# A mixer block of one core: weights of the second half split during the first, and the convolution divided among three engines

## The chip, the cores and the metric

The kernel runs on one core of one Trainium2 chip. Its time is the device time of one execution in microseconds. Before the change the runs took 3051.74, 3052.08 and 3052.36 us; their median is 3052.08.

## What is computed

The reference is two residual blocks over 2048 tokens of 1024 features, in float32.

```python
x = x + gate * gla_mixer(rmsnorm(x, g) * (1 + scale) + shift)     # first block, linear attention in chunks of 64
x = rmsnorm(x, final_g)
u = rms_norm(h) * (1 + scale) + shift                             # second block; h is the first one's output
p = u @ w_in                                                      # q, k, v, z of attention, a and g of the convolution, z of the convolution
attn = attend(rope(q), [k_ctx, rope(k)], [v_ctx, v]) * silu(z_a)  # 8 heads of 64, 2304 keys
y = depthwise_conv31(a * sigmoid(g)) + conv_b                     # 512 channels, 31 taps along the tokens
conv = (silu(layer_norm(y)) @ w_pw + b_pw) * silu(z_c)
h = h + gate * (concat(attn, conv) @ w_out)
```

## The kernel before

The program runs six phases one after the other, each with its own tiles and semaphores and a barrier ahead of it: modulation, the linear attention (`gla_block`), context keys, the projections (`projections`), the attention (`attention`) and the output. A matrix product in float32 is made of three products of rounded values: w_hi by a_hi, w_hi by a_lo and w_lo by a_hi, where hi is the rounded value and lo what is left. ScalarE rounds (`w_hi` from `w_raw`), GpSimd subtracts (`w_lo`).

**Turns.** Tokens go in four blocks of 512 (`NB`). In a block, each turn of TensorE multiplies one tile of weights, 1024 x 128, by the block: 24 matmuls of 512 columns into one of two banks. The linear attention has 32 turns a block (0 to 7 for q and k, 8 to 15 for v, 16 to 23 for the gate, 24 to 31 for the output), the projections 22 (0 to 7 for a and g of the convolution in turn, 8 to 13 for q, k and v, 14 to 21 for the two z). ScalarE evicts the bank of turn j, which TensorE needs again in turn j+2 (waits on `proj_out` and on `evac`).

**Weights.** In block 0 of both phases SyncE loads a raw tile, the two parts are formed, and SyncE stores them to scratch (`keep_split`). In later blocks it loads the pair of tile n from scratch into one of three buffers, two turns ahead (`load_pair`, L324 and L1088), once turn n-3 is done. All of SyncE's transfers stand in one queue written out by hand, in order of the turns, with the waits of each between them.

**Convolution.** Four groups of 128 channels. The gate (L1358) writes u into `conv_in`; VectorE then makes 31 taps a group (`tap`, L1330 the first, L1333 the others), each one multiply-add of 128x528 into `conv_acc`. `TAPS_OF_TURN` deals the 124 taps of a block to its turns; 28 are carried into the first four turns of the next block, and in the end behind the last turn. VectorE also forms u of the next block in turns 9 to 19 (L1317, L1319 the rounded part, L1321 the rest), does q's norm and rotation, and gates z. GpSimd adds the squares of h (L1059) and two products of q (L1161, L1167).

**Attention.** 32 steps, one for each head and block of queries, of 18 key tiles each. TensorE makes scores (L1598, L1599), the scores for the maxima of the next step (`piece`, L1558, four banks, 20 pieces in groups of four), and the weighted sum of v (L1573). ScalarE takes the exponentials (L1662). VectorE takes the maxima from PSUM (L1694), writes them to `mz` (L1703), splits q (L1687) and adds the last two of eight pairs to the denominator (L1711) and halves it (L1715). GpSimd adds the first six pairs (L1543, 128x1024). ScalarE's and GpSimd's steps are loops with registers for most steps.

## Time and profile before

| | us |
|---|---|
| median of the three runs | 3052.08 |
| the profiled execution, its own time | 3046.05 |
| its span, first to last instruction | 3044.2 |
| TensorE busy | 2615.0 (86%) |
| VectorE busy | 1814.0 (60%) |
| ScalarE busy | 1092.1 (36%) |
| GpSimd busy | 793.3 (26%) |
| mean granted clock of TensorE | 0.928 of full |

Busy times are unions of the instructions of an engine. Engine names of the rows are PE (TensorE, with PEld for its weight loads), DVE (VectorE), ACT (ScalarE), POOL (GpSimd) and SP (SyncE); SPq is SyncE issuing a transfer. In a row of a timeline x13 are 13 instructions in a row, and the bracket holds the idle time ahead of them and what ended it. A number like L1333 is a line of the kernel before.

### The profile page before, as it was taken

The page shows a single profiled execution, that of the slowest core. Times are in us where ns is not written, and L with a number is a line of the kernel's source. Part 1 is how long each engine was busy: PE and PEld are TensorE (multiplying, and loading weights), DVE is VectorE, ACT ScalarE, POOL GpSimd, SP SyncE. Part 2 cuts the span into 40 slices and gives each one's busy share as a digit, 9 for nine tenths or more (in the row PEclk, how much of TensorE's full clock was granted, in tenths as well). Part 3 has the DMA queues.
Part 4 walks back from the last instruction along what each step waited for, and adds up shares of the span by engine and source line. Part 5 has one row for each costly group of instructions (what it writes and reads, how often), then busy time and mean ns, then how long its engine had stood idle before and what let it go on. Part 6 is the DMA issues. An engine that isn't in the chain of part 4 may idle for free. (4 is left out here: it accounts for less than half of the span.)

```text
span 3044.2 us, 35493 instructions
## 1 busy us (share of the span) xinstructions
PE 2615.0 (86%) x11647; PEld 1777.7 (58%) x11647; DVE 1814.0 (60%) x2830; ACT 1092.1 (36%) x1875; POOL 793.3 (26%) x365
## 2 busy tenths in 40 slices
PE   8599899999999962767989797299999999975998
PEld 1277677777777751645767675144454445433776
DVE  0106423533532524698898888677777777746564
ACT  0234433333332413241414132144454445433332
POOL 0033300000000101532111111166566656642000
PEclk9799999999999985888999999599999999987999
DMA  8275664454355341746555554411111111124334
GB/s 307 94 250 167 225 218 143 155 186 164 134 193 193 101 152 59 258 150 228 188 185 202 183 204 157 99 27 26 33 26 28 27 33 26 28 71 149 117 117 148
DMA packets 230581, 414.82 MB, mean 136 GB/s; under 512 B 19607, under 2 KB 112397, under 8 KB 230204
## 3 DMA queue, kind: packets, MB, share of 16 engines
q1 hardware_dynamic: 230096, 413.13, 40.9%
q8 instruction: 70, 1.15, 0.2%
q14 instruction: 51, 0.42, 0.0%
q10 hardware_dynamic: 364, 0.13, 0.0%
HBM read 306.87 MB, written 97.94 MB: 133 GB/s over the span
## 5 line engine op out<-in xcount | busy, mean ns | idle before, releaser
L1694 DVE TENSOR_REDUCE att_mx<-att_bank_m 128x1 f32<-128x512 f32 (+1 forms) x640 | 365.5, 630 | 111.6 <-PE att_bank_m L1558 107.6
L1662 ACT ACTIVATE att_p_f<-att_bank_s 128x512 f32<-128x512 f32 x576 | 317.7, 598 | 288.0 <-PE att_bank_s L1599 281.0
L412 PE MATMUL gla_bank_g<-gla_a_hi,gla_w_hi 128*128 128x512 f32 x1024 | 416.1, 406 | 4.1 <-POOL gla_w_lo L365 3.1
L412 PE MATMUL gla_bank_g<-gla_a_hi,gla_w_lo 128*128 128x512 f32 x1024 | 403.7, 394 | 0.0
L412 PE MATMUL gla_bank_g<-gla_a_lo,gla_w_hi 128*128 128x512 f32 x1024 | 403.7, 394 | 0.0
L1543 POOL TENSOR_TENSOR att_den<-att_den,att_p_f 128x1024 f32<-128x1024 f32 x160 | 379.4, 2371 | 34.1 <-ACT att_p_f L1662 22.0
L1333 DVE SCALAR_TENSOR_TENSOR proj_conv_acc<-proj_conv_in,proj_conv_w,proj_conv_acc 128x528 f32<-128x528 f32 x508 | 383.2, 825 | 0.3
L1196 PE MATMUL proj_bank_g<-proj_u_hi,proj_w_hi 128*128 128x512 f32 x704 | 302.8, 430 | 74.9 <-DMA proj_w_lo<-scratch_w_lo 37.8
L1196 PE MATMUL proj_bank_g<-proj_u_lo,proj_w_hi 128*128 128x512 f32 x704 | 283.5, 403 | 0.0
L1196 PE MATMUL proj_bank_g<-proj_u_hi,proj_w_lo 128*128 128x512 f32 x704 | 282.6, 401 | 0.0
L1573 PE MATMUL att_bank_o<-att_p_f,att_v 128*64 128x512 f32 x1152 | 268.4, 601 | 0.0
L1598 PE MATMUL att_bank_s<-att_q_a,att_k_a 128*128 128x512 f32 x576 | 258.8, 449 | 1.0 <-ACT att_q_b L1645 1.0
L1599 PE MATMUL att_bank_s<-att_q_b,att_k_b 65*128 65x512 f32 x576 | 230.2, 400 | 0.0
L412 PEld LDWEIGHTS gla_bank_g<-gla_a_hi,gla_w_hi 128*128 128x128 f32 x1024 | 195.3, 191 | 55.6 <-issue 14.2
L412 PEld LDWEIGHTS gla_bank_g<-gla_a_hi,gla_w_lo 128*128 128x128 f32 x1024 | 194.9, 190 | 42.6
L412 PEld LDWEIGHTS gla_bank_g<-gla_a_lo,gla_w_hi 128*128 128x128 f32 x1024 | 195.6, 191 | 38.1 <-issue 0.7
L1196 PEld LDWEIGHTS proj_bank_g<-proj_u_hi,proj_w_hi 128*128 128x128 f32 x704 | 138.6, 197 | 125.2 <-DMA proj_w_lo<-scratch_w_lo 41.0
L1598 PEld LDWEIGHTS att_bank_s<-att_q_a,att_k_a 128*128 128x128 f32 x576 | 109.7, 190 | 136.9 <-issue 105.4
L372 POOL TENSOR_TENSOR gla_ke<-gla_qk,gla_tmp 128x512 f32<-128x512 f32 x16 | 20.8, 1297 | 631.8 <-ACT gla_tmp L610 631.8
L778 DVE COPY gla_v_tok<-gla_bank_t 128x512 f32<-128x512 f32 x32 | 22.1, 691 | 266.6 <-PE gla_bank_t L519 266.6
L1558 PE MATMUL att_bank_m<-att_k_a,att_q_c 64*128 64x512 f32 (+1 forms) x640 | 121.9, 433 | 60.7 <-ACT att_k_a L1634 57.7
L1196 PEld LDWEIGHTS proj_bank_g<-proj_u_lo,proj_w_hi 128*128 128x128 f32 x704 | 138.9, 197 | 35.8 <-issue 8.2
(322 smaller groups left out, 4195.4 us busy)
## 6 DMA issues: line engine op xcount, KB each, us to landing
gla_w_hi<-scratch_w_hi SPq DMA_DIRECT2D x96, 512.0 KB, 3.7
gla_w_lo<-scratch_w_lo SPq DMA_DIRECT2D x96, 512.0 KB, 4.7
proj_w_hi<-scratch_w_hi SPq DMA_DIRECT2D x66, 512.0 KB, 3.9
proj_w_lo<-scratch_w_lo SPq DMA_DIRECT2D x66, 512.0 KB, 5.3
scratch_w_hi<-gla_w_hi SPq DMA_DIRECT2D x32, 512.0 KB, 3.2
scratch_w_lo<-gla_w_lo SPq DMA_DIRECT2D x32, 512.0 KB, 4.2
mod_wslab<-in_ada_w SPq DMA_DIRECT2D x6, 2048.0 KB, 11.2
mod_wslab<-in_w_mod SPq DMA_DIRECT2D x6, 2048.0 KB, 8.1
```

Source lines behind the costliest of these rows:

```text
L372: pool.tensor_tensor(ke[:], qk[:, 1, :, tok(t)], tmp[:, 1, :].rearrange("p (h i) -> p h i", h=4), ALU.mult).then_inc(qs_pool, 1)
L412: last = pe.matmul(banks[s % 2][:], w[:, k, :], a[:, k, :], start=(k == 0 and n == 0), stop=(k == KT - 1 and n == 2))
L778: dve.tensor_copy(v_tok[:, :, tok(j)], T[j % 2][:].rearrange("p (t i) -> p t i", t=NT)).then_inc(v_copied, 1)
L1196: last = pe.matmul(G[j % 2][:], w[:, k, :], a[half][:, k, :], start=(k == 0 and n == 0), stop=(k == KT - 1 and n == 2))
L1333: dve.scalar_tensor_tensor(conv_acc[:, c, :], src, conv_w[:, c, k:k + 1], conv_acc[:, c, :], ALU.mult, ALU.add).then_inc(taps, 1)
L1543: pool.tensor_tensor(den[s][:], pair(0) if j == 1 else den[s][:], pair(j), ALU.add).then_inc(den_pool, 1)
L1558: pe.matmul(M[p % MBANKS][:, 0:width], q_c[s][rows, P * qt:P * (qt + 1)], k_a[g][rows, TB * n:TB * n + width], start=True, stop=True).then ...
L1573: last = pe.matmul(O[HD * half:HD * (half + 1), :], v[g][:, 2 * j + half, :], p_f[:, 2 * j + half, :], start=(j == 0), stop=(j == NPR - 1))
L1598: pe.matmul(S[kt % SBANKS][:], k_a[g][:, keys], q_a[s][:], start=True, stop=False)
L1599: pe.matmul(S[kt % SBANKS][:], k_b[g][:, keys], q_b[s][:], start=False, stop=True).then_inc(s_done, 1)
L1662: act.activation(p_f[:, kt, :], S[kt % SBANKS][:], ACT.Exp, scale=float(HD) ** -0.5).then_inc(p_done, 1)
L1694: dve.reduce_max(mx[:, qt, n:n + 1], M[p % MBANKS][:, 0:min(TB, KEYS - TB * n)], AX_X).then_inc(mx_read, 1)
```

## The change

Four things change. (1) The 22 tiles of the second block's input weights are rounded, their remainders formed and both stored to scratch during blocks 1 to 3 of the linear attention, one tile in every second turn from 0 to 14 (8, 8 and 6 tiles), through one buffer each (`w2_hi`, `w2_lo`). The projections load all their weights from scratch, into four buffers, on ScalarE's queue. (2) Of the four channel groups VectorE keeps two, 62 taps a block, of 512 columns and 528 in the last block. GpSimd takes group 0 in the projections, a multiplication and an addition for each tap. Group 3 is gated into `vraw` and stored as `conv_u`; in the attention ScalarE multiplies it by a tap's weight, four 512-wide parts a step, and GpSimd adds 128x2048. (3) ScalarE writes u_hi. (4) Block 3 no longer forms u for a block that follows. The steps of ScalarE and GpSimd in the attention are written out.

```diff
 gla_block
+    LATER_EVERY, LATER_PER = 2, 8
+    def later_tile(b, j):
+        n = LATER_PER * (b - 1) + j // LATER_EVERY
+        return n if b and j >= 0 and j % LATER_EVERY == 0 and j < LATER_EVERY * LATER_PER and n < len(IN2_COLS) else None
...
+        w2_hi, w2_lo = sb("w2_hi", [P, KT, P], F32R), sb("w2_lo", [P, KT, P], F32R)
...
+                def load_later(m):
+                    if m >= 2:
+                        sp.wait_ge(w2_rest, UP + m - 1)
+                    else:
+                        sp.wait_ge(w_rest, UP + NW - 1 + m)
+                    sp.dma_start(w_raw[m % 2][:], w_in2[:, :, IN2_COLS[m]:IN2_COLS[m] + P]).then_inc(w_landed[m % 2], 16)
+                def keep_later(m):
+                    sp.wait_ge(w2_rest, UP + m + 1)
+                    for part, tile in (("w2_hi", w2_hi), ("w2_lo", w2_lo)):
+                        sp.dma_start(d[part][m], tile[:].rearrange("p k n -> p (k n)").bitcast(F32)).then_inc(w2_kept, 16)
...
                         load(b * NW + j + 2)
+                        m = later_tile(b, j)
+                        if m is not None:
+                            load_later(m)
+                        m = later_tile(b, j - 3)
+                        if m is not None:
+                            keep_later(m)
...
+                def later_rest(b, j):
+                    m = later_tile(b, j)
+                    if m is not None:
+                        pool.wait_ge(w2_rounded, UP + m + 1)
+                        pool.tensor_tensor(w2_lo[:], w_raw[m % 2][:], w2_hi[:].bitcast(F32), ALU.subtract).then_inc(w2_rest, 1)
...
+                    m = later_tile((n - 1) // NW, (n - 1) % NW)
+                    if m is not None:
+                        act.wait_ge(w_landed[m % 2], UP + 16 * (NW // 2) + 16 * (m // 2) + 16)
+                        act.wait_ge(w2_kept, UP + 32 * m)
+                        act.activation(w2_hi[:], w_raw[m % 2][:], ACT.Copy).then_inc(w2_rounded, 1)
...
 projections
-    NTAP = 4 * TAPS
-    TAPS_OF_TURN = [10, 10, 8] + [0] * 2 + [8] * 5 + [2] * 6 + [8] * 4 + [6] * 2
-    CARRIED = sum(TAPS_OF_TURN[:4])
+    RING = 4
+    NTAP = 2 * TAPS
+    POOL_C, DVE_C, LATE_C = 0, 1, 3
+    TAPS_OF_TURN = [6, 5] + [0] * 4 + [7] * 3 + [5] * 2 + [0] * 5 + [2, 3, 3, 4, 5, 3]
+    CARRIED = sum(TAPS_OF_TURN[:6])
+    POOL_TAPS_OF_TURN = [0] * 2 + [2] * 2 + [1] * 4 + [3, 2, 3, 2, 3] + [1] * 6 + [2] * 2
...
+        def window(b):
+            return CW if b == NB - 1 else TB
...
-                        if b == 0:
-                            keep_split(j)
-                        load(b * NW + j + 2)
...
+                            for k in range(done, done + POOL_TAPS_OF_TURN[j]):
...
+                                    pool.tensor_scalar(prod[:, 0:window(b)], conv_src(b, POOL_C, k), conv_w[:, POOL_C, k:k + 1], None,
+                                                       ALU.mult).then_inc(pool_prod, 1)
+                                    pool.wait_ge(pool_prod, UP + b * (TAPS - 1) + k)
+                                    pool.tensor_tensor(acc, acc, prod[:, 0:window(b)], ALU.add).then_inc(pool_taps, 1)
...
+                def load_pair(n):
+                    j = n % NW
+                    for part, tile in (("w2_hi", w_hi[n % RING]), ("w2_lo", w_lo[n % RING])):
+                        act.dma_start(tile[:].rearrange("p k n -> p (k n)").bitcast(F32), d[part][j]).then_inc(pair_landed[n % RING], 16)
+                for n in range(RING):
+                    load_pair(n)
...
+                def round_u(b, k):
+                    act.wait_ge(hm, UP + b * 8 + k + 1)
+                    act.activation(u_hi[b % 2][:, k, :], hbuf[:, k, :], ACT.Identity, bias=modv[:, 1, k:k + 1]).then_inc(u_done_hi, 1)
...
                         act.wait_ge(proj, UP + b * NW + j + 1)
+                        if b * NW + j + RING < NB * NW:
+                            load_pair(b * NW + j + RING)
...
 attention
+    MUL_AT = (4, 6, 8, 13)
...
+                def tap(k):
+                    pool.wait_ge(conv_mul, UP + NB * (k + 1))
...
+                        pool.tensor_tensor(conv_acc[:].rearrange("p (a b) -> p a b", a=NB), former, conv_prod[:, k % 2, :, :], ALU.add).then_inc(conv_taps, 1)
...
                         pool.tensor_tensor(den[s][:], pair(0) if j == 1 else den[s][:], pair(j), ALU.add).then_inc(den_pool, 1)
-                steps(pool, body)
+                    if i < TAPS:
+                        tap(i)
...
+                    act.activation(conv_prod[:, k % 2, part, :], conv_in[:, k + TB * part:k + TB * (part + 1)], ACT.Copy,
+                                   scale=conv_w[:, k:k + 1]).then_inc(conv_mul, 1)
...
+                        if kt in MUL_AT and i < TAPS:
+                            multiply(i, MUL_AT.index(kt))
```

## Rows read from the trace of the kernel before

**Rows 1.** Stretches, us: PE, PEld, DVE, ACT, POOL busy; PEclk, DMA share, GB/s

```profile
103.00:1127.00 1024.00, 941.98 (x4562) 738.20 (x4561) 397.86 (x762) 370.50 (x697) 128.94 (x66) 0.96 0.51 171
...
1209.00:1433.50 224.50, 155.60 (x578) 114.93 (x578) 184.10 (x209) 66.03 (x88) 84.95 (x37) 0.83 0.60 200
1433.50:1586.00 152.50, 138.41 (x554) 107.54 (x554) 135.06 (x187) 46.80 (x68) 27.33 (x17) 0.95 0.57 191
...
1744.50:1896.00 151.50, 134.24 (x530) 103.90 (x530) 135.11 (x188) 45.99 (x67) 25.30 (x17) 0.93 0.51 177
1896.00:1941.00 45.00, 0.00 (x0) 0.00 (x0) 33.23 (x49) 0.69 (x2) 0.31 (x1) 0.55 0.27 100
1941.00:2720.00 779.00, 750.91 (x3456) 376.54 (x3456) 577.75 (x927) 377.69 (x676) 465.34 (x194) 0.97 0.13 32
```

**Rows 2.** Costliest groups: busy us, mean ns | idle before, releaser

```profile
L1333 DVE SCALAR_TENSOR_TENSOR proj_conv_acc<-proj_conv_in,proj_conv_w,proj_conv_acc 128x528 f32<-128x528 f32 x508 | 383.2, 825 | 0.3
```

**Rows 3.** Waits of TensorE, 1209 to 1433.5: us, times, longest

```profile
PE proj_bank_g L1196 <- POOL proj_w_lo L1146: 23.9, 5, 11.3
```

**Rows 4.** Timelines of the projections, VectorE then GpSimd: start, us, instructions

```profile
1247.44 8.91 DVE L1333 SCALAR_TENSOR_TENSOR proj_conv_acc<-proj_conv_in,proj_conv_w,proj_conv_acc 128x528 f32<-128x528 f32 x13
...
1382.74 9.85 DVE L1333 SCALAR_TENSOR_TENSOR proj_conv_acc<-proj_conv_in,proj_conv_w,proj_conv_acc 128x528 f32<-128x528 f32 x5
...
1174.83 7.08 POOL L1141 MEMSET proj_conv_in<- 128x8380 f32 x1 [134.86 <-POOLq L1061]
...
1250.56 10.91 POOL L1146 TENSOR_TENSOR proj_w_lo<-proj_w_raw,proj_w_hi 128x1024 fp32r<-128x1024 f32 x2 [4.97 <-ACT proj_w_hi L1227]
...
1385.72 1.75 POOL L1161 TENSOR_TENSOR proj_qraw<-proj_qraw,proj_qsin 128x512 f32<-128x512 f32 x1
1387.43 1.77 POOL L1167 TENSOR_TENSOR proj_qraw<-proj_qraw,proj_cos 128x512 f32<-128x512 f32 x1
...
1461.49 1.28 POOL L1059 TENSOR_TENSOR proj_hrs<-proj_hrs,proj_ht 128x512 f32<-128x512 f32 x1 [0.85 <-ACT proj_ht L1232]
```

**Rows 5.** Linear attention: timeline; group of roundings; DMA issues with median landing

```profile
415.34 0.60 ACT L629 ACTIVATE gla_qk<-gla_bank_g 128x512 f32<-128x512 f32 x1 [5.74 <-PE gla_bank_g L412]
...
420.78 0.32 SPq L324 DMA_DIRECT2D gla_w_hi<-scratch_w_hi  x1
421.14 0.43 SPq L324 DMA_DIRECT2D gla_w_lo<-scratch_w_lo  x1
...
L573 ACT ACTIVATE gla_w_hi<-gla_w_raw 128x1024 fp32r<-128x1024 f32 x31 | 32.8, 1057 | 30.3 <-DMA gla_w_raw<-in_gla_w_out 28.5 <-DMA gla_w_raw<-in_gla_w_in 1.7
...
gla_w_lo<-scratch_w_lo SPq DMA_DIRECT2D x96, 512.0 KB, 4.7
scratch_w_lo<-gla_w_lo SPq DMA_DIRECT2D x32, 512.0 KB, 4.2
```

**Rows 6.** Timeline of TensorE: first and last of a turn's 24 matmuls

```profile
1600.68 0.80 PE L1196 MATMUL proj_bank_g<-proj_u_hi,proj_w_hi 128*128 128x512 f32 x1 [3.89 <-DMA proj_w_lo<-scratch_w_lo]
...
1607.38 0.39 PE L1196 MATMUL proj_bank_g<-proj_u_hi,proj_w_lo 128*128 128x512 f32 x1
```

**Rows 7.** Timelines of one attention step: GpSimd, VectorE, TensorE

```profile
2265.63 4.82 POOL L1543 TENSOR_TENSOR att_den<-att_den,att_p_f 128x1024 f32<-128x1024 f32 x2 [0.76 <-ACT att_p_f L1662]
2278.52 2.37 POOL L1543 TENSOR_TENSOR att_den<-att_p_f 128x1024 f32<-128x1024 f32 x1 [8.07 <-ACT att_p_f L1662]
...
2269.18 1.30 DVE L1703 TENSOR_SCALAR att_mz<-att_m 128x4 f32<-128x4 f32 x1
2270.98 1.23 DVE L1711 TENSOR_TENSOR att_den<-att_den,att_p_f 128x1024 f32<-128x1024 f32 x1 [0.50 <-ACT att_p_f L1662]
2272.24 0.69 DVE L1687 TENSOR_TENSOR att_q_a<-att_q_raw,att_q_c 64x512 fp32r<-64x512 f32 x1
...
2274.83 2.48 DVE L1694 TENSOR_REDUCE att_mx<-att_bank_m 128x1 f32<-128x512 f32 x4
...
2278.22 0.73 PE L1558 MATMUL att_bank_m<-att_k_a,att_q_c 64*128 64x256 f32 x4
```

More of the change, by code:

```diff
@@ L28 @@
 GLA_COLS = 3088
+COL_Q, COL_K, COL_V, COL_ZA, COL_A, COL_G, COL_ZC = 0, 512, 640, 768, 1280, 1792, 2304
+IN2_COLS = ([c for i in range(4) for c in (COL_A + P * i, COL_G + P * i)] + [COL_Q + P * i for i in range(4)] + [COL_K, COL_V]
+            + [COL_ZA + P * i for i in range(4)] + [COL_ZC + P * i for i in range(4)])
 VROWS = {}
@@ L1212, in turn @@
                             last.then_inc(vt, 1)
-                        if j == 8:
+                        if j == 8 and b + 1 < NB:
                             sum_h(b + 1)
@@ L1534, in _ @@
                     pool.tensor_tensor(k_b[g][0:HD, :], k_raw[g][0:HD, :], k_a[g][0:HD, :].bitcast(F32), ALU.subtract).then_inc(k_lo_done, 1)
-                def body(i, s, g, before, after):
+                pool.memset(conv_in[:, 0:PAD], 0.0).then_inc(conv_cleared, 1)
+                pool.memset(conv_in[:, PAD + SEQ:], 0.0).then_inc(conv_cleared, 1)
+                def tap(k):
+                    pool.wait_ge(conv_mul, UP + NB * (k + 1))
+                    if k:
+                        pool.wait_ge(conv_taps, UP + k)
+                    former = conv_prod[:, 0, :, :] if k == 1 else conv_acc[:].rearrange("p (a b) -> p a b", a=NB)
+                    if k == 0:
+                        pool.sem_inc(conv_taps, 1)
+                    else:
+                        pool.tensor_tensor(conv_acc[:].rearrange("p (a b) -> p a b", a=NB), former, conv_prod[:, k % 2, :, :], ALU.add).then_inc(conv_taps, 1)
+                for i in range(STEPS):
+                    s = i % 2
                     need(pool, den_sum, i - 1)
@@ L1664, in body @@
                             finish(i - 1, 1 - s)
-                        if kt == 11 and not (isinstance(i, int) and i + 2 >= STEPS):
+                        if kt == 11 and i + 2 < STEPS:
                             round_q(i + 2, s)
```

252 lines of the change are left out of this document (129 added, 123 removed).

## The prediction

> **What bounds the kernel now.** I read the busy times by stage first. In [rows 1] the stretches are, in order: the linear attention (103 to 1127 us), three of the four blocks of the projections (0 from 1209, 1 from 1433.5, 3 from 1744.5 to 1896; block 2 fills the 158.5 us between), what follows their last matmul (to 1941), and the attention (1941 to 2720). The reader is to see three different limits. In the linear attention TensorE is busy 942 of 1024 us. In the attention it is busy 751 of 779. In the projections it is not the limit: a block asks 134 to 138 us of it, but blocks 1 to 3 take 152 to 158 us and VectorE is busy 135 of 152.5 in those shown; block 0 takes 224.5 us, with VectorE busy 184 and TensorE 156. In the 45 us after the last matmul VectorE is busy for 33, with convolution taps. The list of groups says what VectorE does: 508 taps of 128x528, 383 us [rows 2]. The waits of block 0 begin with the remainders of the weights, 23.9 us [rows 3].
>
> Then the timeline of GpSimd and of VectorE, since the change gives GpSimd work in two stages. VectorE alone runs 13 taps in 8.91 us, one each 0.68 us. Beside GpSimd's instructions five take 9.85 us, and GpSimd's 512-wide additions take 1.75 and 1.77 instead of the 1.28 that one takes alone; they start 1.71 apart [rows 4]. So the two take turns: a VectorE instruction that reads two SBUF tensors waits until GpSimd's has ended. One 512-wide GpSimd addition costs a busy VectorE 1.72 - 0.68 = 1.04 us. The same rows show the other outcome: two GpSimd subtractions that met the chain of 13 taps took 10.91 us together and VectorE lost nothing.
>
> **The change, part by part.**
>
> **1. Weights prepared ahead.** Block 0 loses its roundings, remainders, stores and raw loads; its weights come from scratch as in blocks 1 to 3, four tiles ahead, on ScalarE's queue. Its turn then costs what a turn of the other blocks costs.
>
> **2. What this costs in the linear attention.** 22 tiles are treated in turns 0, 2, ... 14 of blocks 1 to 3. By themselves they are a rounding on ScalarE (1.06 us, as in [rows 5]), a subtraction on GpSimd (busy 129 us of the 1024 [rows 1]) and 1.5 MB of transfers, and all could lie beside matmuls. A turn lasts 5.44 us: from the eviction at 415.34, which one turn's end releases, to the pair issue at 420.78, which the next releases [rows 5]. The wait is what costs. w2_hi is one buffer. In turn j ScalarE must see the former tile stored before it rounds, and this stands ahead of its eviction of turn j. SyncE issues that store in its iteration j+1, and ahead of it there stands the wait of the pair load for turn j to be done. So after the end t of turn j come: the pair's two issues and landing, t + 0.36 + 4.7 = t+5.1 [rows 5]; the store's megabyte behind it. Its bounds: it lands 4.2 us after its own issue [rows 5], t+5.5, if it shares nothing, or behind the pair, at the 335 GB/s that 171 GB/s at a share of 0.51 make [rows 1], 3.1 us later, t+8.2. I take the second, since both go through SyncE's queue and the same engines. Then rounding 1.06 and eviction 0.6: t+9.9. TensorE ends turn j+1 at t+5.44 and needs that eviction for turn j+2: it stands 4.5 us. A gap of 3.9 us was followed by a turn of 7.1 us instead of 5.44, its first matmuls at the granted clock's half level of 1.2 GHz [rows 6]; I add 1.5. There are 7, 7 and 5 such waits (the first tile of a block finds its buffer free). Nine in the q and k turns cost 6.0 each; eight in the v turns, which last 0.5 longer, 5.5; the two in turn 14 stand ahead of the decays too (five activations of about 0.6 and a table load, some 4 us of ScalarE), 9.5. Sum 54 + 44 + 19 = **+117**; by the lower bound without a fall of the clock 19 x 1.8 + 8 = +42.
>
> **3. The convolution in the projections.** VectorE keeps two of four channel groups, 62 taps a block for 124: 62 x 0.68 = -42 us; 512 columns for 528 give 1 us more, u_hi on ScalarE 4. What it is busy with falls from 135 to 140 us (the 1.04 for each of 17 GpSimd additions is in that) to about 92. GpSimd gets 31 multiplications and 30 additions a block. The additions take 30 x 1.04 = 31 from VectorE. A multiplication by a scalar is not in this trace. Lower bound: the memset of 8380 columns, 7.08 us [rows 4], 0.84 ns a column, makes 0.43 for 512 and some 0.2 of start, of which VectorE would feel 0.2; upper bound: an addition, 1.04. I take 0.6, between, because it reads one tensor and writes one: 31 x 0.6 = 19. VectorE is back at 92 + 50 = 142. It has next to nothing in turns 2 to 5 (22 us that are TensorE's), and some 130 of the 142 fall into turns 6 to 20, where TensorE asks 6 us a turn and VectorE now 8.7; with the other seven turns at 5.5 that is 168, less the two turns, 11 us, by which TensorE may lead: 157. The Trainium skill, GPSIMD Engine Reference, section 3.1, has a GpSimd loop of at most two operations limited by its ports at 1.03 cycles an element of 1.2 GHz, an estimate of 0.44 us for 512; no row here shows one, and by it the sum would be about 50 us less. So blocks 1 and 2 stay (157 for 152.5 and 158.5). Block 0 becomes one of them: 224.5 - 157 = 67. Block 3 forms no u for a block that isn't there, 24 instructions of 0.5 to 0.75 and the additions and root ahead of them: 20. The carried taps after the last matmul are 11 for 28: 12; the last store is half as long, 2; VectorE, less late there, 4. Sum **-105**. Bounds: TensorE's 134 us in every block, -180; every new GpSimd instruction at 1.04, -50. ScalarE's added pair issues, 0.36 + 0.43 a turn [rows 5], and its rounding of u, a 512-wide operation like the eviction's 0.6, fit beside 5.44 us; if they did not, its evictions would come late (rival d).
>
> **4. The fourth channel group in the attention.** ScalarE multiplies, four times 0.6 us a step, beside matmuls. GpSimd adds 128x2048: 2.41 for 1024 columns (4.82 for two, [rows 7]) make 4.5. It starts when the sixth addition ends, at 2270.5 in the step shown, and fits into GpSimd's 8.07 us of idle. But VectorE has placed its own two-input work in that gap: an addition at 2270.98 (1.23 us), the split of q at 2272.24 (0.69), another addition like the first and a halving of 0.69, then at 2274.83 four maxima in 2.48 us [rows 7]. That GpSimd shuts VectorE out here too is seen at 2269.18: 128x4 elements take 1.30 us, until 2270.48, when GpSimd's pair has just ended. With the tap first, the addition starts at 2275.0, 4.0 us late, the maxima at 2278.8, two of them are read at 2280.1 and four at 2281.3. TensorE's next four score products come at 2278.22 and reuse those banks: 1.9 us, then 0.7, and 0.2 behind: 2.8 us a step. VectorE is busy 578 of 779 us [rows 1], so its later gaps absorb its own lateness before the next tap. 30 taps: 84; the 1 MB store at the end 3: **+87**. Bounds: +3 if VectorE's chain comes first, and +130 if the clock falls each time by 1.5. The longest is half of that in [rows 6], so I add none. The unrolled loops of GpSimd and ScalarE I cost at nothing: ScalarE is busy 378 of 779 us, GpSimd 465 [rows 1], and if instruction fetch stalled one of them it would have to be for microseconds a step.
>
> Sum: 117 - 105 + 87 = **+99**. The profiled execution takes 3046.05 us for a span of 3044.2, so 3145; it is 6 below the median of the runs, 3052.08, which gives **3151 us**.
>
> **The rivals.** (a) Faster: VectorE keeps the port. If a GpSimd instruction is held until VectorE's chain breaks, as the 10.91 us of [rows 4], and the one-input multiplication does not shut VectorE out, the attention loses 3 only and the projections fall to TensorE's 134: 117 - 180 + 3 = -60, **2992 us**. It decides once the projections' gain less the attention's loss passes 120 us. For it: that row; the gap of 8.07. Against: the alternation at 1385 to 1389, and that the tap starts 0.45 us before VectorE's addition. Chance 0.27. (b) The stores land early: item 2 is 42, **3076**. For it: 4.2 us median; against: these had less beside them. 0.12. (c) The clock falls in the attention's waits: +45, **3196**; 0.10. (d) The change does not shorten block 0, because ScalarE, now also issuing, comes late there: +67, **3218**; against it, ScalarE is busy 66 of 224 us there [rows 1]; 0.05. My forecast has the remaining 0.46, with a range of its own of 3095 to 3215.
>
> **The numbers.** What a measurement of this kernel can tell from no change is about 0.2%, 6 us. (a) gives faster 0.27; where (b) meets a projections' gain above mine the two signs cancel, same 0.03; all else is slower, 0.70. The range goes from just under (a) to just over (d), since the bounds of items 3 and 4 reach into both: 2975 to 3225.
>
> **What would show it.** In the linear attention after: a span some 115 longer, TensorE's idle before turns 2, 4, ... by a wait on ScalarE's eviction, and that one on the landing of scratch_w_hi/lo. In the projections: block 0 near 155, VectorE's taps with a mean above 1 us, TensorE's mean granted clock no higher. In the attention: steps 2.8 longer, VectorE's additions of att_den at about 5 us for 1.23 in one of two. The forecast is wrong if the linear attention keeps its 1024 us, if a block falls under 140, or if the attention keeps 779.

## The result, and the profile after

The changed kernel takes 3278.52 us (median of 4 runs, 3275.56 to 3283.29) against 3051.91 us (4 runs, 3049.19 to 3052.36): a ratio of 1.0746, 95% interval 1.0727 to 1.0765. It is slower by 227 us; the forecast was 99 us, with a range for the time of 2975 to 3225 us, and the result lies outside it. The profiled executions are 3283.29 us (span 3281.5) and 3046.05 us (span 3044.2), 237 us apart, and the stages below belong to them.

| from, to | before | after | difference | forecast |
|---|---|---|---|---|
| linear attention, first to last product | 965.1 | 1091.9 | +127 | +117 |
| projections, first product to last tap | 724.4 | 622.2 | -102 | -105 |
| attention, first exponential to the output stage | 756.6 | 975.3 | +219 | +87 |

The rest of the span is 6 us shorter. Two of the three terms come out within 10 us of their forecast; the attention costs 2.5 times its own. The stretches of the kernel after, in the columns of [rows 1] and with its stages (linear attention; projection blocks 0 to 3; what follows their last product; attention):

```profile
101.00:1252.00 1151.00, 981.72 (x4576) 763.10 (x4576) 402.08 (x762) 388.00 (x719) 182.27 (x88) 0.93 0.55 182
1332.40:1487.50 155.10, 138.15 (x554) 105.99 (x555) 116.53 (x116) 55.18 (x80) 126.77 (x78) 0.95 0.54 184
1487.50:1647.50 160.00, 138.57 (x556) 106.93 (x555) 122.78 (x124) 52.05 (x76) 127.58 (x78) 0.95 0.55 191
1647.50:1801.50 154.00, 134.66 (x555) 104.72 (x554) 126.02 (x128) 52.38 (x76) 127.75 (x78) 0.97 0.56 195
1801.50:1943.20 141.70, 132.07 (x553) 103.28 (x551) 101.68 (x107) 38.83 (x56) 114.55 (x71) 0.99 0.53 181
1943.20:1960.00 16.80, 0.03 (x1) 0.00 (x0) 10.64 (x16) 1.08 (x2) 0.00 (x0) 0.58 0.13 48
1960.00:2963.00 1003.00, 897.26 (x3456) 457.85 (x3456) 688.08 (x928) 449.11 (x800) 602.15 (x227) 0.82 0.11 27
```

TensorE is still busy in 897 of the attention's 1003 us, for the same 3456 matmuls that took 751 before. That is the row that says where the time went: only 78 us of the growth are idle time. The granted clock is 0.82 instead of 0.97, and in the linear attention 0.93 instead of 0.96.

**One stall of the linear attention**, timelines of SyncE's queue, ScalarE, GpSimd and TensorE in block 1:

```profile
423.31 0.32 SPq L335 DMA_DIRECT2D gla_w_hi<-scratch_w_hi  x1
423.67 0.43 SPq L335 DMA_DIRECT2D gla_w_lo<-scratch_w_lo  x1
424.15 0.43 SPq L350 DMA_DIRECT2D scratch_w_hi<-gla_w_hi  x1
424.62 0.43 SPq L350 DMA_DIRECT2D scratch_w_lo<-gla_w_lo  x1
...
432.12 1.06 ACT L618 ACTIVATE gla_w_hi<-gla_w_raw 128x1024 fp32r<-128x1024 f32 x1 [9.76 <-DMA scratch_w_lo<-gla_w_lo]
433.08 1.07 ACT L674 ACTIVATE gla_qk<-gla_bank_g 128x512 f32<-128x512 f32 x2
...
433.25 2.37 POOL L398 TENSOR_TENSOR gla_w_lo<-gla_w_raw,gla_w_hi 128x1024 fp32r<-128x1024 f32 x1 [23.15 <-ACT gla_w_hi L618]
...
428.10 0.39 PE L452 MATMUL gla_bank_g<-gla_a_lo,gla_w_hi 128*128 128x512 f32 x1
428.33 0.39 PE L452 MATMUL gla_bank_g<-gla_a_hi,gla_w_lo 128*128 128x512 f32 x1
433.71 0.66 PE L452 MATMUL gla_bank_g<-gla_a_hi,gla_w_hi 128*128 128x512 f32 x1 [5.00 <-ACT gla_qk L674]
...
436.73 0.63 PE L452 MATMUL gla_bank_g<-gla_a_lo,gla_w_hi 128*128 128x512 f32 x1
437.16 0.47 PE L452 MATMUL gla_bank_g<-gla_a_hi,gla_w_lo 128*128 128x512 f32 x1
```

The turn before ends at t = 423.31, where the next pair load goes out. The stores follow at 424.15 and 424.62. ScalarE has been idle for 9.76 us when the second has landed, 8.8 us after t (forecast 8.2), rounds, and only then evicts; TensorE stands 5.0 us (forecast 4.5). Then its matmuls start 0.43 us apart (436.73 to 437.16) and not 0.23 as before the stall (428.10 to 428.33): the granted clock is at its half level for 3.4 us. [rows 5] has the same places without the stall.

**One step of the attention**, timelines of GpSimd, VectorE and TensorE, the places of [rows 7]:

```profile
2307.99 4.91 POOL L1612 TENSOR_TENSOR att_den<-att_den,att_p_f 128x1024 f32<-128x1024 f32 x2 [5.15 <-ACT att_p_f L1753]
2312.84 4.60 POOL L1603 TENSOR_TENSOR att_conv_acc<-att_conv_acc,att_conv_prod 128x2048 f32<-128x2048 f32 x1
...
2311.62 1.31 DVE L1786 TENSOR_SCALAR att_mz<-att_m 128x4 f32<-128x4 f32 x1
2313.42 5.11 DVE L1794 TENSOR_TENSOR att_den<-att_den,att_p_f 128x1024 f32<-128x1024 f32 x1 [0.49 <-ACT att_p_f L1753]
2318.56 0.69 DVE L1770 TENSOR_TENSOR att_q_a<-att_q_raw,att_q_c 64x512 fp32r<-64x512 f32 x1
2319.28 1.23 DVE L1794 TENSOR_TENSOR att_den<-att_den,att_p_f 128x1024 f32<-128x1024 f32 x1
2320.54 0.69 DVE L1798 TENSOR_TENSOR att_den<-att_den 128x512 f32<-128x512 f32 x1
2321.15 2.47 DVE L1777 TENSOR_REDUCE att_mx<-att_bank_m 128x1 f32<-128x512 f32 x4
...
2322.49 0.50 PE L1628 MATMUL att_bank_m<-att_k_a,att_q_c 64*128 64x256 f32 x2 [1.76 <-DVE att_mx L1777]
2323.68 0.50 PE L1628 MATMUL att_bank_m<-att_k_a,att_q_c 64*128 64x512 f32 x2 [0.69 <-DVE att_mx L1777]
```

GpSimd's 128x2048 addition starts 0.58 us ahead of VectorE's, which takes 5.11 us where [rows 7] has 1.23; the next three follow 3.9 us late, then the maxima, and TensorE waits for them twice, 1.76 and 0.69 us. All of this is near the forecast. What was not is in the windows behind it (columns as above):

```profile
2313.00:2324.00 11.00, 8.55 (x38) 4.17 (x38) 10.48 (x9) 5.86 (x11) 6.84 (x2) 1.00 0.18 48
2324.00:2332.00 8.00, 8.00 (x30) 5.77 (x30) 3.77 (x8) 3.98 (x7) 5.10 (x3) 0.57 0.07 16
2332.00:2350.00 18.00, 17.76 (x78) 7.72 (x74) 14.77 (x18) 8.64 (x16) 11.26 (x4) 1.00 0.06 15
2350.00:2366.00 16.00, 13.61 (x40) 7.81 (x42) 8.64 (x16) 5.20 (x10) 9.46 (x4) 0.57 0.09 25
```

After the waits the granted clock is at its lower level of 1.2 GHz for most of 8 us, and it comes back before the next step's waits put it there again. From step 2 to step 31, in the same columns, before and after:

```profile
2016.20:2692.80 676.60, 670.25 (x3132) 335.70 (x3132) 524.68 (x840) 334.08 (x608) 412.67 (x174) 1.00 0.11 28
```

```profile
2037.80:2928.20 890.40, 813.60 (x3134) 416.64 (x3132) 631.25 (x842) 400.88 (x726) 544.39 (x204) 0.83 0.09 21
```

To three digits the second is 0.833: on average 10.2 of the 30.7 us of a step are at the half level, which costs 5.1 us. The waits of TensorE are 2.65 us a step for 0.22. The step before, the added waits and the clock make 23.3 + 2.4 + 5.1 = 30.8, and the step is 30.7. The loss differs from step to step although the waits do not: all 29 steps have two waits of 1.7 to 1.8 and 0.4 to 0.7 us, and they last 29.2 to 32.1 us, with 6.8 to 13.7 us at the half level.

### The profile page after: what moved, and what is told of

Its sections match the earlier page's. It is cut to its first block and busy times, and to the rows that moved or that the text cites. A ratio compares the mean times of both kernels' runs of the same rounds, so it can differ in the third digit from the quotient of the medians.

```text
span 3281.5 us, 34614 instructions
## 1 busy us (share of the span) xinstructions
PE 2776.8 (85%) x11645; PEld 1870.5 (57%) x11645; DVE 1775.2 (54%) x2494; ACT 1173.8 (36%) x2019; POOL 1302.8 (40%) x634
## 5 line engine op out<-in xcount | busy, mean ns | idle before, releaser
L452 PE MATMUL gla_bank_g<-gla_a_hi,gla_w_hi 128*128 128x512 f32 x1024 | 429.4, 419 | 37.6 <-ACT gla_qk L674 33.5
L1233 PE MATMUL proj_bank_g<-proj_u_hi,proj_w_hi 128*128 128x512 f32 x704 | 293.5, 417 | 11.9 <-DVE proj_u_lo L1365 8.4
L1643 PE MATMUL att_bank_o<-att_p_f,att_v 128*64 128x512 f32 x1152 | 303.3, 667 | 0.0
L1668 PE MATMUL att_bank_s<-att_q_a,att_k_a 128*128 128x512 f32 x576 | 293.3, 509 | 1.0 <-ACT att_q_b L1715 1.0
L1669 PE MATMUL att_bank_s<-att_q_b,att_k_b 65*128 65x512 f32 x576 | 260.7, 453 | 0.0
L398 POOL TENSOR_TENSOR gla_w_lo<-gla_w_raw,gla_w_hi 128x1024 fp32r<-128x1024 f32 x22 | 52.1, 2366 | 518.5 <-ACT gla_w_hi L618 518.5
L1376 DVE SCALAR_TENSOR_TENSOR proj_conv_acc<-proj_conv_in,proj_conv_w,proj_conv_acc 128x512 f32<-128x512 f32 (+1 forms) x240 | 246.9, 1093 | 0.0
L1628 PE MATMUL att_bank_m<-att_k_a,att_q_c 64*128 64x512 f32 (+1 forms) x640 | 147.4, 498 | 102.6 <-DVE att_mx L1777 73.3
L1204 POOL TENSOR_SCALAR proj_prod<-proj_conv_in,proj_conv_w 128x512 f32<-128x512 f32 (+1 forms) x120 | 229.1, 1909 | 8.2
L1794 DVE TENSOR_TENSOR att_den<-att_den,att_p_f 128x1024 f32<-128x1024 f32 x64 | 194.1, 3033 | 28.0 <-ACT att_p_f L1753 16.3
L1668 PEld LDWEIGHTS att_bank_s<-att_q_a,att_k_a 128*128 128x128 f32 x576 | 127.6, 222 | 140.0 <-issue 109.9
```

The costliest lines, as they stand in the source:

```text
L452: last = pe.matmul(banks[s % 2][:], w[:, k, :], a[:, k, :], start=(k == 0 and n == 0), stop=(k == KT - 1 and n == 2))
L1204: pool.tensor_scalar(prod[:, 0:window(b)], conv_src(b, POOL_C, k), conv_w[:, POOL_C, k:k + 1], None, ALU.mult).then_inc(pool_prod, 1)
L1233: last = pe.matmul(G[j % 2][:], w[:, k, :], a[half][:, k, :], start=(k == 0 and n == 0), stop=(k == KT - 1 and n == 2))
L1376: dve.scalar_tensor_tensor(acc, conv_src(b, c, k), conv_w[:, c, k:k + 1], acc, ALU.mult, ALU.add).then_inc(taps, 1)
L1643: last = pe.matmul(O[HD * half:HD * (half + 1), :], v[g][:, 2 * j + half, :], p_f[:, 2 * j + half, :], start=(j == 0), stop=(j == NPR - 1))
L1668: pe.matmul(S[kt % SBANKS][:], k_a[g][:, keys], q_a[s][:], start=True, stop=False)
```

## The experiments

Each run is named by its label. Where several attention runs are compared, the figures are a mean over the 29 steps from the start of step 2 to that of step 31, and the waits are TensorE's whole idle time in them. Those timed in rounds have an interval; the others are one execution each, beside the kernel before on the same chip.

### The two costs, each taken away

**e1_no_conv_in_attention**: in the attention neither ScalarE's multiplies nor GpSimd's additions.

> Leaves out channel group 3's whole convolution (the 31x4 multiplies on ScalarE and the 30 additions on POOL in the attention); what is stored for that group is its input. All else is the changed kernel, with the attention's programs of POOL and ScalarE still written out step by step instead of in a loop. Theory P (the addition on POOL keeps VectorE off SBUF, PE waits, and its clock falls to half in each step): the attention's step goes from 30.3 us back to 23.4 us, the attention from 975 to about 760 us, and the kernel from 3278 to about 3062 us. Rival A (the multiplies on ScalarE) expects the same here. Rival L (the cost lies in the programs without a loop, or in the two loads at the attention's start) expects that under half of the 219 us goes: 3170 us or more. My forecast's own size of this part, 87 us, would give 3191 us.

Measured 3070.30 us (ratio 1.0064, 1.0048 to 1.0081); step 23.3 us, clock 1.00, attention 761.7 us. This is theory P's number within 8 us. L is out: the programs without a loop cost nothing a step, and the attention is only 5 us longer than in the kernel before. Half of that is the end, with the 1 MB store (36.2 us from the last step's start, for 33.6 in the kernel before and in e9, which has no such store). The other half is the first step, 25.7 for 22.9 us, and it is not the added loads: e9, which has none of them, takes 25.8 us there. Both have 16 us at the half level in it, where the kernel before has 10.

**e2_addition_after_fold**: the same work, with GpSimd's addition later by one place.

```diff
+                    if i:
+                        pool.wait_ge(den_dve, UP + i * DVE_ADDS)
+                        tap(i - 1)
                     need(pool, den_sum, i - 1)
...
-                    if i < TAPS:
-                        tap(i)
```

> The same 30 additions of 128x2048 on POOL and the same multiplies, but POOL makes the addition of step i at the start of step i+1, once VectorE has folded the denominators, instead of between its own last denominator addition and VectorE's first. VectorE then has nothing but sources in PSUM until the next step's end. Theory P: VectorE's 5.1 us addition is back at about 1.23 us, the step is 23.4 to 24.5 us, the clock in the attention 1.00, the attention 760 to 795 us, the kernel 3060 to 3100 us. Rival Q (POOL has simply too much to do in a step, 18.8 of 23.4 us) and rival A (ScalarE's multiplies) expect the step to stay over 27 us and the kernel over 3180 us.

Measured 3091.34 us (ratio 1.0131, 1.0114 to 1.0148); step 24.0, clock 1.00. 30 additions of 4.56 us are there, nothing is done less, and 187 us are gone: GpSimd's load and ScalarE's multiplies (rivals Q and A) are not the cause, the place of the addition is. Timelines of GpSimd, VectorE and TensorE in one step:

```profile
2210.74 4.56 POOL L1603 TENSOR_TENSOR att_conv_acc<-att_conv_acc,att_conv_prod 128x2048 f32<-128x2048 f32 x1 [4.54 <-DVE att_den L1798]
...
2217.78 12.44 POOL L1615 TENSOR_TENSOR att_den<-att_den,att_p_f 128x1024 f32<-128x1024 f32 x5
...
2210.58 2.48 DVE L1777 TENSOR_REDUCE att_mx<-att_bank_m 128x1 f32<-128x512 f32 x4
...
2228.32 1.93 DVE L1786 TENSOR_SCALAR att_mz<-att_m 128x4 f32<-128x4 f32 x1
2230.34 1.23 DVE L1794 TENSOR_TENSOR att_den<-att_den,att_p_f 128x1024 f32<-128x1024 f32 x1
...
2230.30 0.65 PE L1635 MATMUL att_bank_m<-ident_sb,att_mz 128*65 128x128 f32 x4 [0.85 <-DVE att_mz L1786]
```

The addition starts when the fold at 2209.97 (the halving of the denominator) has ended, and VectorE's maxima, which read PSUM, run through it in the 2.48 us that they take without it. What remains, 0.7 us a step, is a wait of TensorE for a 128x4 operation of VectorE, which ends only when GpSimd's last denominator addition does, now 0.7 us later.

**e3_weights_every_4_turns**:

```diff
-    LATER_EVERY, LATER_PER = 2, 8
+    LATER_EVERY, LATER_PER = 4, 8
```

> One number changed in the linear attention: a weight tile of the projections is rounded in every fourth turn of blocks 1 to 3 and no longer in every second, so that its two stores have four turns to land before ScalarE needs their buffer. The same 22 roundings, remainders, loads and stores. Theory S (the wait of ScalarE for the stores, and PE's half clock behind it): nearly all of the 127 us goes, the linear attention is back within 15 us of the kernel before (965 us from its first to its last product), and the kernel is at 3150 to 3170 us. Rival W (the work itself: 22 roundings on ScalarE, 22 remainders on POOL that keep VectorE off SBUF, and the traffic of the stores) expects at most half of it to go: 3215 us or more.

Measured 3191.26 us (ratio 1.0467, 1.0449 to 1.0484); linear attention 999.1 us: 93 of the 127 us gone, where 112 or more were expected. Rival W (at most half) is out, but 34 us are left. The starts of the turns place them: in blocks 1 and 2 turn 29 lasts 15.0 for 7.4 us and the next some 1.5 more, and in blocks 1 to 3 turns 16, 20 and 24 lose 1.6 to 1.9 us each. Most stand beside tiles in turns 28, 16, 20 and 24 (block 3 has none in 24). So some 93 us are the wait for the buffer; that the rest is in where a tile falls is an inference from these places, which e14 below bears out.

**e4_both**: both edits.

> Both edits: the addition on POOL after the fold, and a weight tile every fourth turn. If the two costs are independent they add up: about 3278 - 115 - 205 = 2958 us, which is faster than the kernel before by some 94 us, near the 102 us that the projections gained. If one edit only moves a wait, it is over 3000 us.

Measured 3004.00 us, ratio 0.9845 (0.9828 to 0.9861): 1.6% faster than the kernel before. The two savings alone, 187 and 87 us, would give 3004 as well, so the costs are independent. My 2958 was too low by what e2 and e3 had left.

### Lateness, ScalarE and the size of a piece

**e5_vector_late_3** and **e6_vector_late_1**: the kernel before, with additions of unused data on VectorE.

```diff
                         if kt == 17:
+                            for late in late_out:
+                                dve.tensor_tensor(late[:], late_in[:], late_in[:], ALU.add)
                             add_den(i, s, NPR - 2)
```

> The kernel before, with three additions of 128x1024 in SBUF (1.23 us each, results unused) put on VectorE at the end of each attention step, ahead of the denominator addition of line 1711: VectorE is 3.7 to 3.9 us late as in the changed kernel (4.0 us), with nothing added on POOL or ScalarE. Theory C (lateness of VectorE makes a wait of PE of under 3 us, and the half clock that follows costs more than the wait): the step goes from 23.35 to 29 to 31 us, the attention from 757 to 940 to 990 us, the kernel to 3235 to 3290 us, and the clock in the attention alternates. Rival N (the lateness costs its 2.8 us a step and the clock stays, as I forecast; the rest of the changed kernel's 7.0 us comes from POOL or ScalarE): step 26.2 us, kernel 3140 us.

> As the run with three additions, with one: VectorE is 1.25 us late in each step. By my forecast's slack (4.0 us late gave 2.8 us of wait, so 1.2 us are free) this costs nothing and the step stays at 23.3 to 23.6 us, the kernel at 3045 to 3060 us. If any wait of PE, however short, brings the half clock, the step is 25 us or more and the kernel 3100 us or more.

Measured 3178.84 us with three and 3047.38 us with one, beside 3052.43 us. The first fell between the theories: step 27.4 us where C had 29 to 31 and N 26.2. Its timeline says why (VectorE, then TensorE):

```profile
2225.18 3.48 DVE L1755 TENSOR_TENSOR att_late_out<-att_late_in 128x1024 f32<-128x1024 f32 x3
2228.59 1.21 DVE L1714 TENSOR_TENSOR att_den<-att_den,att_p_f 128x1024 f32<-128x1024 f32 x1
...
2233.76 0.50 PE L1561 MATMUL att_bank_m<-att_k_a,att_q_c 64*128 64x256 f32 x2 [0.69 <-DVE att_mx L1697]
2234.95 0.51 PE L1561 MATMUL att_bank_m<-att_k_a,att_q_c 64*128 64x512 f32 x2 [0.69 <-DVE att_mx L1697]
```

The three take 3.48 us, and VectorE's own wait of 0.5 us ahead of its addition takes up the first part, so it is 2.8 us late and not 3.7 (1.80 us from the 128x4 operation's start to the addition's in the kernel before, 4.59 here); TensorE waits twice 0.69 us. The clock is 0.906, which costs 2.6 us a step: the two waits together are 1.4 and what follows them 2.6. So C has the mechanism and N does not: lateness of VectorE alone, without a tap, lowers the clock, and on average the half level costs more than the waits. Not in every step: three of the 29 have the same two waits and no time at the half level. With one addition nothing waits and nothing is lost, as expected.

**e7_multiplies_alone**: ScalarE's 124 multiplies without GpSimd's additions.

> Leaves out the 30 additions of channel group 3 on POOL; ScalarE's 124 multiplies of 128x512 in the attention stay (0.73 us each, 2.9 us a step), and what is stored for the group is its input. Theory P: they go into ScalarE's idle time, the step is 23.4 to 23.9 us and the kernel within 15 us of the run with neither (3070 us). Rival A (the multiplies delay the exponentials and with them PE): the step is over 26 us and the kernel over 3150 us.

Measured 3067.16 us, step 23.3 us. Rival A is out: e1, without the multiplies, has the same step.

**e8_addition_in_four**: the addition of 128x2048 as four of 128x512 in the old place.

> The changed kernel with the addition of a tap cut into four of 128x512 (1.15 us each), in the same place behind POOL's last denominator addition. If VectorE gets SBUF between two pieces, its addition is late by 1.2 us and not 4.0, its next ones by as much again, and the step is 24 to 28 us (kernel 3090 to 3215 us). If POOL's pieces follow one another without letting it in, all is as with one piece: step 30.3 us, kernel 3278 us.

Measured 3186.30 us, step 27.6 us, clock 0.93. GpSimd and VectorE:

```profile
2222.32 7.42 POOL L1604 TENSOR_TENSOR att_conv_acc<-att_conv_acc,att_conv_prod 128x512 f32<-128x512 f32 x4
...
2222.90 1.78 DVE L1796 TENSOR_TENSOR att_den<-att_den,att_p_f 128x1024 f32<-128x1024 f32 x1 [0.51 <-ACT att_p_f L1755]
2224.71 1.67 DVE L1772 TENSOR_TENSOR att_q_a<-att_q_raw,att_q_c 64x512 fp32r<-64x512 f32 x1
2226.41 2.19 DVE L1796 TENSOR_TENSOR att_den<-att_den,att_p_f 128x1024 f32<-128x1024 f32 x1
2228.64 1.65 DVE L1800 TENSOR_TENSOR att_den<-att_den 128x512 f32<-128x512 f32 x1
```

VectorE is let in between two pieces, and the time lies in the range given for that case. They alternate: four pieces take 7.42 us for 4.6, and each of VectorE's four operations is lengthened by 0.5 to 1.0 us. VectorE is late by 3.4 us at the end and TensorE waits 2.05 us more a step than in the kernel before (the changed kernel: 2.43); only the clock is better (0.927 for 0.833).

The attention runs side by side, us a step:

| run | waits of TensorE | granted clock | lost at the half level | step |
|---|---|---|---|---|
| before | 0.22 | 1.000 | 0 | 23.3 |
| e6, e7 | 0.21, 0.22 | 1.000 | 0 | 23.3 |
| e2 | 0.92 | 1.000 | 0 | 24.0 |
| e10 (below) | 1.04 | 1.000 | 0 | 24.1 |
| e5 | 1.59 | 0.906 | 2.6 | 27.4 |
| e8 | 2.27 | 0.927 | 2.0 | 27.6 |
| after | 2.65 | 0.833 | 5.1 | 30.7 |

(Lost is one minus the clock, times the step.) e8 waits more than e5 and loses less, so the loss is no fixed multiple of the waits. Nor is it one within a run: 27 steps of e8 take 27.1 to 27.5 us and two take 31.6 and 30.5, with nearly the same two waits. What decides it stays open.

### What the projections gained, and what they still lose

**e9_weights_alone**: the projections and the attention of the kernel before, with block 0 loading finished pairs, and the linear attention of e3.

> The weights part without the convolution part: linear attention with a tile every fourth turn as in the run before, the projections and the attention of the kernel before, but for the projections' block 0, which loads the finished pairs like the later blocks. Linear attention +34 us (999 against 965); block 0 of the projections from 201.6 to about 155 us, as in the changed kernel (-46), all else as before: about 3038 us. By my forecast's own size for block 0 (-67 us) it is 3016 us. If block 0 is held by VectorE's taps once the weights are out of it, it stays over 180 us and the kernel is over 3060 us. Below 3000 us the convolution's new places would be worth nothing, since both edits together took 3004 us.

Measured 3028.85 us, ratio 0.9921 (0.9902 to 0.9940). I had expected 3038 us. The projections take 681.0 us for 724.4, so of the 102 us the weights are 43. The other 59 are all else that changed there: the convolution's new places above all, but also u_hi on ScalarE, the u that block 3 no longer forms, and the loads through ScalarE's queue. These were not taken apart. With e2's place for the addition (e4) these 59 cost some 27 us in the attention; in the changed kernel they cost 219.

**e12_no_taps_on_pool**: 30 of GpSimd's 31 taps a block left out of the projections.

> The changed kernel without 30 of the 31 taps of channel group 0 in the projections (their 120 multiplies and 120 additions on POOL); the group's stored result holds the first tap alone. By my forecast these are hidden behind PE in all blocks: the projections from first product to last tap stay at 622 us within 6 us and the kernel at 3270 to 3285 us. Rival: they keep VectorE off SBUF and so hold its taps and the turns; then 15 us or more go and VectorE's taps fall from 1.09 us towards 0.7 us.

Measured 3201.86 us: 77 us less, all in the projections (544.6 us). My forecast had these taps hidden, and they were not. First comes block 1 of e12, from its first product to the next block's; then groups of all blocks, VectorE's taps and GpSimd's multiplications in the changed kernel, and VectorE's taps in e12.

```profile
1467.00:1601.40 134.40, 130.90 (x555) 103.35 (x555) 91.73 (x124) 51.81 (x76) 27.62 (x18) 1.00 0.65 227
```

```profile
L1376 DVE SCALAR_TENSOR_TENSOR proj_conv_acc<-proj_conv_in,proj_conv_w,proj_conv_acc 128x512 f32<-128x512 f32 (+1 forms) x240 | 246.9, 1093 | 0.0
...
L1204 POOL TENSOR_SCALAR proj_prod<-proj_conv_in,proj_conv_w 128x512 f32<-128x512 f32 (+1 forms) x120 | 229.1, 1909 | 8.2
```

```profile
L1373 DVE SCALAR_TENSOR_TENSOR proj_conv_acc<-proj_conv_in,proj_conv_w,proj_conv_acc 128x512 f32<-128x512 f32 (+1 forms) x240 | 166.7, 761 | 0.0
```

The block is 134.4 us, of which TensorE is busy 130.9, at a granted clock of 1.00; the changed kernel has 160.0 at 0.95. The projections of e12 as a whole are 180 us below those of the kernel before, which is the lower bound of my item 3. By the turns' starts 22 of the 26 us lie in turns 10 to 15, above all turn 13: 17.9 us in blocks 0 to 2 of the changed kernel, 7.8 in e12. There TensorE stands 8 to 9 us for VectorE's work on q, which runs late beside GpSimd's taps (timelines of TensorE, VectorE and GpSimd):

```profile
1590.45 2.05 PE L1239 MATMUL proj_bank_r<-proj_qraw,proj_rot_t 128*128 128x512 f32 x2 [8.08 <-DVE proj_qsin L1419]
...
1568.92 0.68 DVE L183 TENSOR_TENSOR proj_qt<-proj_qms,proj_qrs 128x512 f32<-128x512 f32 x1
1569.63 1.65 DVE L185 SCALAR_TENSOR_TENSOR proj_qt<-proj_qt,proj_qrs 128x512 f32<-128x512 f32 x1
1571.40 0.98 DVE L187 SCALAR_TENSOR_TENSOR proj_qrs<-proj_qt,proj_qrs 128x512 f32<-128x512 f32 x1
...
1570.84 1.88 POOL L1204 TENSOR_SCALAR proj_prod<-proj_conv_in,proj_conv_w 128x512 f32<-128x512 f32 x1
1572.80 1.50 POOL L1207 TENSOR_TENSOR proj_conv_acc<-proj_conv_acc,proj_prod 128x512 f32<-128x512 f32 x1
```

**e13_projection_multiplies_on_scalar**: e4, with the products of those taps from ScalarE.

> The run with both edits (3004 us), and in the projections the 120 multiplies of channel group 0's taps on ScalarE instead of POOL, into a ring of five buffers; POOL keeps the 120 additions. Theory P (POOL's taps hold VectorE off SBUF; the multiplies are 58 of their 100 us in a block): VectorE's taps go from 1.09 us towards 0.95, the projections from 622 to about 577 us (58 % of the 77 us that all of POOL's taps cost), the kernel to about 2959 us (2945 to 2975). Rival E (ScalarE's evictions are then late behind the multiplies of 0.73 us, or PE waits for POOL's q and k additions in either case): the projections stay over 605 us and the kernel over 2987 us.

Measured 2990.61 us, ratio 0.9805 (0.9776 to 0.9834); projections 608.0 us. A miss: 14 us of the 45, and both numbers are those of rival E. VectorE's taps went only from 1.09 to 1.03 us and GpSimd's additions rose from 1.41 to 1.57. Turn 13 is even longer, 19.5 us for the 17.4 to 17.9 of e4, with 10.7 us of wait for VectorE's work on q. Whether ScalarE's added work has a part in that was not tried by itself.

**e16_taps_away_from_q_turns** and **e17_same_with_pools_multiplies**: the taps dealt out otherwise, on e15 and e14 below.

```diff
-    TAPS_OF_TURN = [6, 5] + [0] * 4 + [7] * 3 + [5] * 2 + [0] * 5 + [2, 3, 3, 4, 5, 3]
+    TAPS_OF_TURN = [6, 5] + [0] * 4 + [7, 6, 5, 3, 3] + [0] * 5 + [3, 4, 4, 5, 6, 5]
-    POOL_TAPS_OF_TURN = [0] * 2 + [2] * 2 + [1] * 4 + [3, 2, 3, 2, 3] + [1] * 6 + [2] * 2
+    POOL_TAPS_OF_TURN = [0] * 2 + [2] * 8 + [1] * 6 + [2] * 4 + [1]
```

> The best run so far (2959 us) with the same taps dealt out otherwise over the turns of a projection block: VectorE has 24 of its 62 in turns 6 to 10 (31 before) and 27 in turns 16 to 21 (20 before); POOL has 9 of its 31 in turns 8 to 12 and 3 in turns 13 to 15 (13 and 3 before), the others in turns 2 to 7 and 16 to 20. If PE's wait in turn 13 comes from the place of the taps (VectorE arrives 12 us late at the work on q): turn 13 falls from 19.5 us to under 12, each of blocks 0 to 2 from 150 to 138 to 143 us, the projections from 604 to about 575 us, the kernel to about 2930 us. If it is the sum of the taps, the wait only moves: 590 us or more, the kernel over 2945 us.

> The same dealing out, with the multiplies on POOL as in the changed kernel (2975 us with the old dealing out, its projections 622 us). POOL's taps take 3.3 us a pair here, so 9 pairs in turns 8 to 12 are 30 us of the 32 us of those turns: I expect a part of the gain, 600 to 612 us for the projections and 2952 to 2968 us for the kernel.

Measured 2951.76 us (ratio 0.9670, 0.9654 to 0.9686) and 2991.66 us (0.9793, 0.9777 to 0.9810). In e16 turn 13 fell to 13.3 us, but in blocks 1 and 2 turn 1 rose to 16.6 and 11.9 us, where TensorE now waits up to 11.0 us for ScalarE's eviction: 7 us of the expected 29. That wait is only in part a matter of VectorE's load. In block 1 VectorE itself is idle for 12.9 us, until 1379.1, when a store of z has landed. SyncE, whose queue issues that store, had stood 13.8 us for VectorE's last u_lo; it then loads the next h (2 MB, at 1361.26) and stores z behind it (at 1362.36). Another order in that queue was not tried. In e17, 17 us slower than with the old dealing and outside the expected 2952 to 2968, a third wait stands at turn 8 (13 to 16 us); in block 1 it is 9.7 us for GpSimd's sum of the squares of h. So the wait moves with the taps, and I did not find a dealing without one.

### The linear attention again

**e11_store_one_turn_sooner**: the changed kernel, with `later_tile(b, j - 2)` for the store in place of `j - 3`.

> The changed kernel with its tile in every second turn, but SP issues the two stores one turn sooner (some 5.4 us). Theory S (ScalarE waits for the landing of these stores, 4.5 us in a turn of 5.4): the waits go almost wholly, the linear attention is at 970 to 990 us from its first to its last product and the kernel at 3155 to 3180 us. Rival W (the added work on ScalarE and POOL): 1060 us or more and over 3245 us.

Measured 3188.28 us; linear attention 995.1 us. What a stalled q or k turn loses falls from some 5 us to 1.6 or nothing, with the tile in every second turn as before: theory S holds, though both numbers are 5 to 8 us above its ranges, and 97 us were the landing of the stores. Of the 30 us left most are at turn 15, 25.3 and 21.7 us in two blocks for 14.4.

**e10_three_turns_and_split**, **e14_seven_tiles_and_sooner_stores**, **e15_all_three**: attempts at a better version. e10 has a tile every third turn and the addition in two pieces. e14 is e4 with e11's stores and tiles in turns 0 to 12:

```diff
-    LATER_EVERY, LATER_PER = 4, 8
+    LATER_AT = {1: (0, 2, 4, 6, 8, 10, 12), 2: (0, 2, 4, 6, 8, 10, 12), 3: (0, 2, 4, 6, 8, 10, 12, 16)}
```

e15 is e14 with e13's multiplies.

> An attempt at a better version: a weight tile every third turn (so none in turns 24 to 31), and the addition of a tap in two pieces, 128x1536 after the fold and 128x512 behind POOL's fourth denominator addition, where POOL was idle 0.7 us. Tap 0 is written by ScalarE straight into the sum. Theory S: the linear attention is at 975 to 985 us (999 with four turns, which still lost some 19 us at turn 28). Theory P: VectorE's last product of a step is back at 1.3 us (2.0 with the whole addition after the fold), the step at 23.4 to 23.7 us (24.03). Kernel 2955 to 2990 us. If three turns are too few for the stores, the linear attention is over 1020 us and the kernel over 3010 us.

> The run with both edits, but the weight tiles in turns 0, 2, ..., 12 of blocks 1 to 3 (and turn 16 of block 3), their stores issued one turn sooner. From the rows of the runs: three turns a block that cost 1.0 to 1.6 us each, none of the 7 to 11 us at turns 15 and 16, 2 us at turn 16 of block 3: the linear attention at 975 to 985 us from its first to its last product (1004 with a tile every fourth turn), the kernel at 2975 to 2990 us. If the tile of turn 12 alone brings the loss at turn 15, it is over 995 us and the kernel over 2998 us.

> The edits of the two runs before this one together. If they are independent: 3004 - 45 - 24 = 2935 us (2925 to 2965).

Measured: e10 3030.37 us (0.9925, 0.9903 to 0.9947), a miss on both parts: tiles in turns 15 and 21 cost 7 us each and a little in every other, so the linear attention takes 1025.1 us; and the second piece between the denominator additions delayed the last of them as before, so the step is 24.1 us, with one wait of 1.0 to 1.3 us in each and the clock at 1.00. e14 2974.95 us (0.9758, 0.9742 to 0.9775), linear attention 975.8 us, as expected. e15 2958.62 us (0.9699, 0.9682 to 0.9715), within its range. The best version is e16, 3.3% faster than the kernel before.

## Why the prediction was wrong, point by point

**Item 2, the linear attention (+117, measured +127): the mechanism right, the sum nearer than its parts.** The chain of store, landing, rounding and eviction is the one of the trace, 8.8 us for 8.2; e3 and e11 each took away over 90 us of it by giving the stores time. Within the sum, I had 88 us of waits and 28 for the clock. The trace has 126 us at the half level for 31 before, so 48 for the clock, and 79 for waits: the clock was 20 too low, the waits 9 too high, and that they partly cancel is luck.

**Item 3, the projections (-105, measured -102): the sum right by luck, the reason not.** The parts came out at -46 for block 0, -7, -4 and -18 for the others, -27 behind the last product. The 67 I gave to block 0 were measured from a stretch that reached past its end; from product to product it was 201.6 us. GpSimd's taps took less from VectorE than I thought (it is busy 117 to 126 us in blocks 0 to 2, forecast 142), but they took it where TensorE waits for VectorE, at turns 10 to 15, and not as an even load. e12 shows what that was worth: 77 us on top of the 102.

**Item 4, the attention (+87, measured +219): the failed step.** It was "The longest is half of that in [rows 6], so I add none": the fall of the clock at nothing. The mechanism up to TensorE's wait was right and nearly right in size, 3.9 us late for 4.0 and 2.4 us of waits for 2.8. But the clock fell in every step and cost 5.1 us on average, twice the waits, 153 us over 30 steps. e5 shows it without any tap; e2 shows it gone with all of the work still there. I had put aside [rows 6] because a single wait of mine was shorter than 3.89 us, which was no argument: no row of the kernel before shows what follows two short waits in every step. An upper bound of 1.5 us a step was then no bound: it priced a step as having one short fall, and on average 10.2 us of each step are spent at the half level.

**The rivals.** (c), the clock in the attention, was the right one, with 0.10 and 45 us; it cost 153 us. (a) is refuted by the attention's timeline: GpSimd's addition started first and VectorE waited it out. The Trainium skill, SBUF — State Buffer, section "SBUF: two separate sides", states this as an exclusive lock which the instruction that starts first holds to its end; the trace agrees, 5.11 us for 1.23. (b) is refuted by the stores' landing at t + 8.8, and (d) by block 0's 155.1 us.

## What to carry to other kernels

Where TensorE is the bound and runs at its full clock, a new wait can cost more than its length: here 2.4 us of waits a step cost 7.4 and 1.4 us cost 4.1. It need not: where the one wait that each step has grew by 0.7 or 0.8 us (e2, e10), that cost no more than itself. So give the fall of the clock a term with both bounds, and not a rival's chance. Place an addition of GpSimd behind VectorE's last work on two SBUF tensors, where VectorE reads from PSUM: the same 30 additions cost 214 us in one place and 22 in the next (attention 975, 783 and, without them, 762 us). And when a stage comes out at the forecast sum, take its parts away one by one all the same; 77 us were hidden in a term whose sum was right.

## What the runs showed of the hardware that was not expected

- Two waits of 0.69 us a step, some 1.2 us apart (e5), were followed by half-level stretches in most steps, mean clock 0.906. One wait a step left it at 1.00, though it was longer than either of these: 0.85 to 1.16 us in e2, 1.00 to 1.29 in e10.
- GpSimd's multiply by a scalar, with one SBUF input, is dearer than its addition of two: in the changed kernel the shortest of 120 took 1.56 us, with VectorE idle, and the mean is 1.91, where the additions have 1.26 and 1.41. I had bounded its hold on VectorE at 0.2 to 1.04 us. By the Trainium skill, GPSIMD Engine Reference, section 3.1, which has a loop of at most two operations at 1.03 cycles an element, it would be an estimate of 0.44 us; no run here shows it near that, and the measurement decides.
- Cutting the addition into four did not let VectorE finish in time, 3.4 us late at the end for 3.9: the pieces and VectorE's operations take turns and lengthen each other (e8).
- A 128x4 operation of VectorE lasts 1.3 us in the kernel before and 1.9 us in e2: in both it ends when GpSimd's addition of 128x1024 ends (2270.48 and 2270.45; 2230.25 and 2230.22).
